# A ring of nine row slots instead of ten, half of one query-weight group kept on chip, and three more row additions a tile on VectorE

## The reference

```python
def block(xb):
    q = (xb @ w_query).reshape(tb, PEER_HEADS, 2, PEER_KEY_DIM // 2)
    s = jnp.einsum('thpd,pnd->thpn', q, sub_keys)
    top_s, top_i = lax.top_k(s, k)                      # k = 16, twice, of 128 keys
    cand_s = top_s[:, :, 0, :, None] + top_s[:, :, 1, None, :]
    cand_i = top_i[:, :, 0, :, None] * PEER_N_KEYS + top_i[:, :, 1, None, :]
    best_s, best_j = lax.top_k(cand_s.reshape(tb, PEER_HEADS, k * k), k)
    idx = jnp.take_along_axis(cand_i..., best_j, axis=-1)
    gate = jax.nn.softmax(best_s, axis=-1)
    u = expert_u[idx]
    act = jax.nn.gelu(jnp.einsum('thkd,td->thk', u, xb))
    return jnp.einsum('thk,thkd->td', gate * act, expert_v[idx])
```

## Time and profile before

| | |
|---|---|
| median of 3 runs | 1569.57 us (1568.6 to 1571.91) |
| profiled execution | 1567.15 us, of it span 1565.6 us |
| TensorE busy | 1336.1 us (85%), granted clock 0.951 over the span |
| VectorE busy | 1076.9 us (69%) |
| ScalarE busy | 650.1 us (42%) |
| GpSimd busy | 551.9 us (35%) |
| DMA | 615.71 MB, mean 393 GB/s |

### The profile page before, as it was taken

How to read it: one execution, slowest core, us unless ns; L and a number is a source line. 1 busy time by engine, 2 the same in 40 slices (tenths; PEclk the granted TensorE clock), 3 DMA queues, 4 the chain that set the end, 5 groups by cost and what they waited for, 6 DMA issues and landing times.

```text
span 1565.6 us, 14973 instructions
## 1 busy us (share of the span) xinstructions
PE 1336.1 (85%) x4112; PEld 638.6 (41%) x4112; DVE 1076.9 (69%) x2621; ACT 650.1 (42%) x1910; POOL 551.9 (35%) x581
## 2 busy tenths in 40 slices
PE   8999999798888699989979689789989687778786
PEld 7755554353433244434444244333436232233332
DVE  2155876776777776768776775868877777767765
ACT  1133443354446345443443444534434444444443
POOL 0035434334343333324243333233343244333431
PEclk9999999999999999989989899899989999999999
DMA  7611999999999999999999999999999999999996
GB/s 271 246 55 70 427 426 426 427 427 427 426 427 426 406 394 427 427 427 424 427 427 427 426 414 427 427 427 396 426 409 427 427 427 426 427 427 426 428 426 272
DMA packets 87271, 615.71 MB, mean 393 GB/s; under 512 B 11371, under 2 KB 11627, under 8 KB 12694
## 3 DMA queue, kind: packets, MB, share of 16 engines
q0 software_dynamic: 76032, 553.68, 84.2%
q1 hardware_dynamic: 11158, 61.09, 9.6%
HBM read 613.69 MB, written 1.05 MB: 393 GB/s over the span
## 4 chain that ended last, share of the span: by engine, by line
PE 42%; DMA 29%; DVE 11%; issue 6%; ACT 4%; POOL 1%; DVEq 0%; POOLq 0%; ACTq 0%
DMA arena<-peer_uv,idx 29%; PE bank L1143 25%; PE bank L722 7%; DVE arena L1944 4%; PE bank L1107 3%; ACT arena L1501 1%; PE bank L1064 1%; ACT L1482 1%; DVE h L1951 1%; PE bank L1190 1%; PE bank L1091 1%; ACT L1477 1%; PE bank L711 1%; POOL arena L666 1%; ACT wgt L1491 1%
## 5 line engine op out<-in xcount | busy, mean ns | idle before, releaser
L1143 PE MATMUL bank<-arena 128*128 128x512 f32 x1940 | 931.6, 625 | 171.3 <-ACT arena L1501 141.7
L1944 DVE CUSTOM_DVE_ANT_0 arena<-arena,bank 128x1024 f32<-128x1024 f32 x528 | 637.0, 1219 | 356.6 <-DMA arena<-peer_uv,idx 344.7
L666 POOL DMA_INDIRECT arena<-peer_uv,idx x528 | 513.1, 972 | 812.2 <-PE bank L1143 733.3
L1143 PEld LDWEIGHTS bank<-arena 128*128 128x128 f32 x1940 | 368.7, 199 | 686.6 <-issue 652.6
L1482 ACT ACTIVATE gl<-dots 128x1 f32<-128x1 f32 x528 | 105.7, 200 | 624.9 <-DVE dots L1944 624.1
L1501 ACT ACTIVATE arena<-con,wgt 128x128 f32<-128x128 f32 x485 | 194.8, 402 | 78.6 <-PE bank L1143 64.1
L1491 ACT ACTIVATE wgt<-gl,gate_e 128x1 f32<-128x1 f32 x528 | 155.5, 295 | 23.3 <-DVE gate_e L1959 3.9
L722 PE MATMUL bank<-wring,hT 128*128 128x512 f32 x256 | 112.5, 592 | 0.0
L722 PEld LDWEIGHTS bank<-wring,hT 128*128 128x128 f32 x256 | 48.5, 190 | 60.3 <-issue 60.3
L1951 DVE SCALAR_TENSOR_TENSOR h<-arena,wgt,h 128x1024 f32<-128x1024 f32 x42 | 53.9, 1283 | 10.7 <-ACT wgt L1491 10.7
L633 POOL TENSOR_TENSOR small<-small,feat_cols 128x1 f32<-128x1 f32 (+2 forms) x12 | 7.8, 652 | 131.1 <-DVEq L1689 59.9
(11 more groups left out here) (228 smaller groups left out, 944.8 us busy)
## 6 DMA issues: line engine op xcount, KB each, us to landing
wring<-gla_in_groups SPq DMA_DIRECT2D x24, 1024.0 KB, 11.4
arena<-peer_uv,idx POOLq DMA_INDIRECT x528, 17.7
wring<-gla_out_groups SPq DMA_DIRECT2D x8, 1024.0 KB, 10.0
wring<-attn_in_groups SPq DMA_DIRECT2D x6, 1024.0 KB, 8.0
gws<-query_groups SPq DMA_DIRECT2D x4, 1024.0 KB, 11.5
wring<-attn_out_groups SPq DMA_DIRECT2D x4, 1024.0 KB, 10.2
wring<-query_groups SPq DMA_DIRECT2D x4, 1024.0 KB, 11.4
kept<-query_groups SPq DMA_DIRECT2D x2, 1024.0 KB, 6.7
```

Of the source, the lines that this page charges most:

```text
L666: nc.gpsimd.indirect_dma_start(out=uvrow[:, slot_of(n), :], out_offset=None, in_=io["peer_uv"].rearrange("l e d -> (l e) d"), in_offset=ba ...
L1143: last = nc.tensor.matmul(yacc[:, 512 * i:512 * i + 512], wdiag[:, k % DIAGS, :], rows_of(g, k, 1)[:, 512 * i:512 * i + 512], start=first, ...
L1944: v.tensor_tensor_reduce(out=rows, in0=rows, in1=xnow, scale=1.0, scalar=0.0, op0=ALU.mult, op1=ALU.add, accum_out=dots[:, g % 2, k:k + 1] ...
```

## The change

The ring has nine slots. A pick's gather goes into slot `n % 9` and waits for pick n - 9; five gathers may start early. The memory that is left, 8 KB a partition, becomes a tile of its own, `kept_more`. In the attention stage it holds `ukv`; when the last product with `ukv` is done (unit `v`, block 0), SyncE loads the first half of the third query group of layer 1 into it, once. `wq1_0` then brings only the second half into `wring`, in both passes, and the queries of layer 1 take the first four of the eight row blocks of this group from `kept_more`. `by_vector` gives picks 1, 5 and 9 to VectorE in tiles 1 to 8 as well.

```diff
-RING = 10
+RING = 9
-FREE_EARLY = 6
+FREE_EARLY = 5
...
+        kept_more = sb("kept_more", [P, RUN])
...
-        ukv = part(arena, (RING - 1) * 2 * D, KV_LORA // P, HALF * 2 * HD)
+        ukv = part(kept_more, 0, KV_LORA // P, HALF * 2 * HD)
...
+        def parts_of(n):
+
+            return (1,) if WEIGHTS[n][0][0] == "wq1_0" else (0, 1)
...
             if g == TILES - 1:
                 return LAST_SHARE
+            if GATHERED[g][0] == 0 and GATHERED[g][1] == 1:
+                return SHARE
             return SHARE if mixer_turn(g)[0] and mixer_turn(g)[1] < len(TENSOR_AT) else ()
...
         def slot_of(n):
 
-            return (n + RING - 1) % RING
+            return n % RING
...
-                for i in range(2):
+                for i in parts_of(n):
                     c = slice(RUN * i, RUN * i + RUN)
                     sp.dma_start(wring[:, n % WSLOTS, c], src[:, c]).then_inc(w_in[n % WSLOTS], 16)
...
+                    wait_front_filled(sp, ("v", 0))
+                    sp.dma_start(kept_more[:, :], io["query_groups"][2][:, 0:RUN]).then_inc(kept_more_in, 16)
...
                     w = query_weights(x // 4, b) if layer else wq0[:, x // 4]
                     for k in range(KC):
-                        last = nc.tensor.matmul(bk(u, at * P, at * P + P), w[:, k, (x % 4) * P:(x % 4) * P + P],
+                        w_k = kept_rows(k) if layer and x < 4 and k < KC // 2 else w[:, k]
+                        last = nc.tensor.matmul(bk(u, at * P, at * P + P), w_k[:, (x % 4) * P:(x % 4) * P + P],
                                                 hT[:, k, b * P:b * P + P], start=(k == 0), stop=(k == KC - 1))
...
+            def kept_rows(k):
+                pe.wait_ge(kept_more_in, 16)
+                return kept_more[:, 512 * k:512 * k + 512]
```

More of the change, by code:

```diff
@@ L290, in build @@
         stat_meta = take(4, HEADS)
-        assert at >= (FREE_EARLY - 1) * 2 * D, at
+        assert at >= FREE_EARLY * 2 * D, at
         prob = take(6, SCORES)
@@ L295, in build @@
         v_mla = take(NB, HALF * HD)
-        assert at <= (RING - 1) * 2 * D, at
+        assert at <= RING * 2 * D, at
         uq = part(kept, 0, Q_LORA // P, HALF * QD)
-        ukv = part(arena, (RING - 1) * 2 * D, KV_LORA // P, HALF * 2 * HD)
+        ukv = part(kept_more, 0, KV_LORA // P, HALF * 2 * HD)
         wq0 = part(gws, 0, 2, KC, 512)
@@ L374, in build @@
         kept_in = sem("kept_in")
+        kept_more_in = sem("kept_more_in")
         filled = [sem(f"filled{i}") for i in UNIT_BANKS]
@@ L715, in weights @@
                 n = GROUP_AT[name]
-                pe.wait_ge(w_in[n % WSLOTS], 32 * (n // WSLOTS + 1))
+                pe.wait_ge(w_in[n % WSLOTS], 16 * sum(len(parts_of(m)) for m in range(n % WSLOTS, n + 1, WSLOTS)))
                 return wring[:, n % WSLOTS, :]
```

## The result

The changed kernel takes 1574.01 us in the median of 10 runs (1569.41 to 1576.16), beside 1570.36 us for the kernel before on the same chip (10 runs, 1566.89 to 1572.56). The ratio is 1.0025, with a 95% interval of 1.0013 to 1.0036: slower by 3.9 us, between 2.0 and 5.7. Run once more, beside e9 and e10, the ratio was 1.0020 (1.0009 to 1.0030), 3.1 us. The prediction was +0.6 us; the time is inside its range, and the size is at the edge of what it called no change (3.1 us).

A forecast was written before the change was run, and what follows sets the result against it. The kernel was taken as bound by its stream of DMA transfers from 150 us on. Terms -4.9 + 0.4 + 2.3 + 1.1 + 0 + 1.7 = +0.6 us gave 1570.2 us, range 1565 to 1575.5 us.

The forecast's parts named there:

- The stream is the bound: From 150 us to the end, time is the bytes transferred, at 2.456 us a MB-sized piece, plus moments the stream runs dry.
- Loads -4.9: One 1 MB query load saved in each GLA pass, where the stream is full: 2 x 2.456 = 4.9 us less.
- The load in front 0: New load into `kept_more`, between the attention's loads and the first gather, where the stream has room: 0.
- Additions 0: VectorE's 24 additions in tiles 1 to 8: neither VectorE nor TensorE sets the pace, so 0 both ways.
- Tile 0, +0.4: Last gather of tile 0 waits for pick 6's mix, goes at 185.7, lands at 191.6, due 191.2: 0.4 us late.
- Tiles 1 and 2, covered: A gather there would land 2.0 us late; the additions bring the release 2.2 us forward: 0, upper end 2.0.
- the rival of +2.6: The additions don't cover tile 2, adding 2.0 us to the forecast: +2.6, 1572.2 us; chance 0.06.
- Tile 10, +2.3: The issue at 572.98 lands at 578.9 where 576.6 is due: 2.3 us late, upper end 2.45.
- Tiles 13, 18, 21: Dry places partly covered by loads of weights: 1.1, 0 and 1.7 us late, each with upper end 2.45.
- The slower rival: Whole gather lost in tiles 10, 13, 18, 21, plus tiles 2 and 0: 12.2 less 4.9, +7.3, 1576.9 us; chance 0.20.
- the fill of the gaps (-4.5): Tiles 13 and 21 filled by weights, tile 10 made up in existing dips: -4.5, 1565.1 us; chance 0.20.
- the way through GpSimd (+24): Each of VectorE's 24 additions delays its gather by 1.0 us in the stream: +24 us, 1594 us; chance 0.04.

The follow-up runs named there:

- e9: Kernel before with ten slots, two of eight row blocks of the third query group kept on chip, VectorE's additions in tiles 1 to 8: -1.9 us against before.
- e10: Changed kernel with nine slots alone: query loads whole, no load in the attention's stage, no additions in tiles 1 to 8: +5.8 us against the kernel before.
- e11: The changed kernel once more, unaltered: +3.1 us against the kernel before.
- e4: Kernel before, ten slots, first half of the third query group not loaded in either GLA pass (output not the reference's): -5.7 us against before.
- e3: Changed kernel, nine slots and additions, with query loads whole again and no load in the attention's stage: +6.0 us against the kernel before.
- e1: Kernel before with ten slots and both query loads, plus only VectorE's additions in tiles 1 to 8: +0.2 us against before.
- e2: Changed kernel without the additions in tiles 1 to 8, nine slots and the quarter kept on chip: +2.2 us against the kernel before.
- e7: Kernel before with ten slots, no additions in tiles 1 to 8, two of eight row blocks of the third query group kept: -1.1 us against before.
- e12: Kernel before with ten slots, whole query loads, no additions in tiles 1 to 8, plus the change's load in the attention's stage: +1.4 us against before.

## Why the prediction was right or wrong

The mechanism held: the kernel is a stream of transfers, and the missing slot costs time where its queue runs dry. The sum, +0.6, was 2.3 us short of the fit's +2.9: 1.2 of it in the slot (no more than the fit's bounds allow for) and 1.3 in the front, less 0.2 in the loads. The slot was mis-sized by more than that in the traces: the dips grew by 8.4 us in the change and 8.8 in e11, where the prediction added up 5.5, and more than 8 us was one of its own signs of being wrong. Another, a dip in tiles 1 and 2, is there in e11 (417 GB/s between gathers 24 and 48) and not in the change (426). That the sum came so near is in part luck, as the places below erred in both directions. By its steps:

- **The stream is the bound.** Right: e4 and the difference of e3 and the change give back the bytes one for one, as nearly as the runs can tell, and a TensorE with 16 us less to do in 200 changes nothing.
- **Loads -4.9.** Right: -5.1 in the fit, and -5.7 in e4 alone.
- **The load in front 0.** The rows showed that the stream has room there, and it has. What they could not show is the clock of TensorE in that stage. Measured +1.4 alone (-0.2 to +2.8) and +1.3 (1.1) in the fit; its cause stays open.
- **Additions 0.** Right: +0.2. Issues of gathers beside an addition take up to 1.95 us in the change (rows below), as in the earlier trace rows, but most are not longer: the 54 that overlap one have a median of 0.95 us. The longest of all, 1.97 us at 908.65, stands beside VectorE's squares for a norm. The Trainium skill ("SBUF — State Buffer", "Who interferes with whom") has a VectorE instruction with two inputs from this memory hold up a GpSimd instruction that reads it: the long issues agree, and the stream does not feel it.

```profile
393.41 1.28 DVE L1966 SCALAR_TENSOR_TENSOR h<-arena,wgt,h 128x1024 f32<-128x1024 f32 x1
...
393.56 1.95 POOL L676 DMA_INDIRECT arena<-peer_uv,idx  x1 [2.17 <-PE bank L1158]
```

For the places, this is how much longer the stretch between the landings of two gathers is than in the kernel before, in us (one profiled execution each, gathers counted from 0, 16 to a tile). Loads of weights and gathers change places at the ends of a stretch, so a single entry can be off by about a gather, and the entries should not be added up.

| gathers | place | e1, e9 (10 slots) | change, e11 | e2, e10 (no additions) | forecast |
|---|---|---|---|---|---|
| 8 to 24 | tile 0 to 1 | 0.2, 1.2 | 3.1, 2.3 | 2.4, 1.9 | 0.4 |
| 24 to 48 | tiles 1, 2 | 0.5, 1.5 | 1.0, 2.9 | 5.5, 4.4 | 0 (without additions up to 2.0) |
| 160 to 176 | tile 10 | -0.6, -0.7 | 1.9, 2.3 | 0.7, 2.4 | 2.3 |
| 204 to 224 | tiles 12, 13 | -0.1, -0.2 | 1.2, 1.6 | 1.9, 2.3 | 1.1 |
| 280 to 304 | tiles 17, 18 | -0.2, 0.0 | 2.8, 2.3 | 1.6, -0.2 | 0 (up to 2.45) |
| 336 to 352 | tile 21 | -0.8, -0.8 | 0.2, -0.2 | -0.6, 0.8 | 1.7 |

A load that changes sides does not count when one takes instead what the slices of the pages lack to 427 GB/s. From the kernel before to the change and e11 this grows by 3.0 and 4.0 us in slices 5 to 7 (tiles 0 to 2, forecast 0.4), by 2.4 and 2.3 in 14 and 15 (tile 10, 2.3), by 2.3 and 2.1 in 19 and 20 (tile 13, 1.1) and by 2.6 and 2.9 in 24 and 25 (tile 18, 0), and it falls by 1.9 and 2.8 in 28 to 30 (tile 21, forecast +1.7; in e1, e7 and e9, with ten slots, it falls there by 1.0 to 1.2 too).

- **Tile 0, +0.4: the step that failed.** In e10 the last gather of tile 0 was issued at 186.26, which is 185.8 less the front's 0.5: the forecast said 185.7. It landed 6.9 us later and not 5.9, so 1.5 us late and not 0.4. The 5.9 us were the least of 528, and the first gather of all; the term should have carried a range: this gather took 5.4 to 7.0 us in the change, e2, e3, e10 and e11. Nor is it the whole loss. In e2, e3 and e11 it lands only 0.3 to 0.5 us later than one gather behind the one before, as forecast, and part of the stretch's loss falls on the first gathers of tile 1 (3.4 and 2.7 us apart in e11), which the prediction did not price. In the change itself the landing took 5.4 us, but the gather was issued later still, at 190.29 with the front 3.0 us late, because a pair of mixes before it took 4.92 us instead of 3.60, at a granted clock of 0.72 from 174.15 to 178.90 us:

```profile
174.15 4.92 PE L1158 MATMUL bank<-arena 128*128 128x512 f32 x8
```

- **Tiles 1 and 2, covered.** Right in part: by the GB/s between gathers 24 and 48 this stretch lacks 3.4 and 3.7 us in e2 and e10, where the prediction had up to 2.0 without the additions, and with them 0.2 in the change, as in the kernel before, and 1.6 in e3 and e11. So the additions gain 1.8 us or more here, and do not always cover the whole, which is the rival of +2.6 in part. Over the whole kernel this gain is not seen: the fit gives the additions 0.0.
- **Tile 10, +2.3.** Right. The issue that the step names, in the change, 5.6 us before its landing, which comes 4.3 us after the landing before, 1.8 more than a gather takes; the rest is lost close by:

```profile
578.62 0.93 POOL L676 DMA_INDIRECT arena<-peer_uv,idx  x1 [7.65 <-PE bank L1158]
```

- **Tiles 13, 18, 21.** Their sum was forecast as 2.8; by the slices the change's two executions have 3.0 and 2.2. Errors offset each other in this: tile 18, set to 0, lost about the whole gather that was its upper end, tile 13 twice its 1.1, and tile 21, set to 1.7, lost nothing. Which of the places the loads of weights fill was not to be had to within a gather.
- **The slower rival** (a whole gather everywhere, +7.3) asked for 12.2 us of loss. The dips grew by 8.4 and 8.8, and +7.3 lies outside the change's interval, so it falls, though it was nearer at tiles 13 and 18; so do the fill of the gaps (-4.5) and the way through GpSimd (+24).

## What to carry to other kernels

In a kernel that is bound by a stream, price a buffer by the places at which the queue runs dry, and check their sum afterwards against the dips: twelve slots to ten left the dips as they were here (11.4 and 11.6 us), ten to nine cost 6.7 us (give or take 1.3), nine to eight some 20 more. Where the forecast of a step is the least of many measured times, carry the spread of the short cases as the term's range. What saves bytes is worth its bytes; take it without giving up a slot (e9) if any room is left beside the ring.

## What was not expected of the hardware

- In tiles 4 to 8 the granted clock is lower where TensorE has fewer mixes: 0.91 in the change and in e1, with TensorE busy 159 to 160 of 200 us and waiting for the stream in between, and 0.97 to 0.98 in the kernel before, e2, e7 and e10, which lack these additions, with 174 to 175 us busy. The engine that is relieved runs more of its time at 1.2 GHz; here the stream hid it. One row of e1:

```profile
320.00:520.00 200.00, 159.61 (x444) 74.48 (x445) 162.33 (x373) 93.57 (x269) 81.95 (x84) 0.91 1.01 427
```

- Nearly all that separates e12's profile from the kernel before's is set in the first 160 us, where the clock's level in the attention's stage differs (0.54 for 1.00 from 100 to 110 us), and not in the 1400 us of stream.
